# Block sums of a two-level MLP product moved from GpSimd to VectorE in a Hymba-style decoder step

## The reference

```python
def _channel_and_ple(h, mix, p_l, w_out, g_ffn, w_up, w_down, w_ple, w_ple_norm, w_ple_gate):
    h = h + mix @ w_out                                   # 2048 x 2048
    u = _rmsnorm(h, g_ffn)
    h = h + jnp.square(jax.nn.relu(u @ w_up)) @ w_down    # 2048 x 8192, 8192 x 2048
    e = _rmsnorm(p_l @ w_ple, w_ple_norm) * jax.nn.sigmoid(h @ w_ple_gate)
    return h + e
# decode state, 16 heads x 64 x 128 for each of 8 sequences:
    st = st * jnp.exp(d_ * a_gj)[..., None, None] + jnp.einsum('bgjp,bgn->bgjpn', x_ * d_[..., None], b_)
```

## Time and profile before

| | |
|---|---|
| median of 3 runs | 2960.68 us (2950.65 to 2961.87) |
| profiled execution | 2962.45 us, span 2960.7 us |
| output projection ends, first unit starts | 1136 us |
| up projection | 1136.7 to 1994.3 us |
| down projection | 2005.3 to 2722.2 us |
| PLE, gate, final norm | to 2960.7 us |
| busy: PE, DVE, ACT, POOL | 88%, 72%, 38%, 49% |

### The profile page before, as it was taken

How to read it: one execution, slowest core, us unless ns; L and a number is a source line. 1 busy time by engine, 2 the same in 40 slices (tenths; PEclk the granted TensorE clock), 3 DMA queues, 4 the chain that set the end, 5 groups by cost and what they waited for, 6 DMA issues and landing times.

```text
span 2960.7 us, 51598 instructions
## 1 busy us (share of the span) xinstructions
PE 2611.2 (88%) x20223; PEld 2465.4 (83%) x20223; DVE 2144.2 (72%) x2523; ACT 1124.8 (38%) x1845; POOL 1455.2 (49%) x778
## 2 busy tenths in 40 slices
PE   7999999967868997888888888886999999999998
PEld 7999999823447996778878888886999999999998
DVE  4287877457476227898888888885999999998533
ACT  3111111247633223444444444442444444444322
POOL 0098899000072015555555555554666666655322
PEclk9999999987778998899999999998999999999999
DMA  4487888498433331444444444457555655552223
GB/s 127 121 284 258 288 302 272 127 415 310 184 100 123 100 115 53 148 149 160 162 147 151 149 160 149 160 186 274 201 188 191 210 201 194 201 172 79 94 93 115
DMA packets 334327, 526.46 MB, mean 178 GB/s; under 512 B 16421, under 2 KB 257699, under 8 KB 324966
## 3 DMA queue, kind: packets, MB, share of 16 engines
q1 hardware_dynamic: 311096, 510.16, 50.1%
q10 hardware_dynamic: 22990, 13.01, 1.5%
HBM read 442.67 MB, written 80.55 MB: 177 GB/s over the span
## 4 chain that ended last, share of the span: by engine, by line
PE 46%; DVE 19%; POOL 14%; DMA 9%; issue 7%; ACT 3%; SPq 2%; ACTq 0%; POOLq 0%; DVEq 0%
DVE wl L2454 9%; PE ps L1479 7%; PE ps L1481 7%; PE ps L1484 7%; PE ps L1894 7%; PE ps L1896 7%; PE ps L1897 7%; POOL sr L1343 5%; DMA rb<-in_w_up 5%; POOL kpage L1245 5%; POOL tb L1366 2%; DMA kpage<-in_cache_k 1%; DMA vpage<-in_cache_v 1%; ACT wh L1068 1%; DVE hst L2479 1%
## 5 line engine op out<-in xcount | busy, mean ns | idle before, releaser
L1479 PE MATMUL ps<-uh,wh 128*128 128x260 f32 x2464 | 651.6, 285 | 18.4 <-DVE wl L1991 13.8
L1481 PE MATMUL ps<-ul,wh 128*128 128x260 f32 x2464 | 647.6, 284 | 0.0
L1894 PE MATMUL ps<-op,wh 128*128 128x260 f32 x1536 | 461.1, 300 | 129.5 <-DVE wl L2454 117.9
L1991 DVE TENSOR_TENSOR wl<-raw,wh 128x1024 fp32r<-128x1024 f32 (+1 forms) x162 | 254.8, 1573 | 360.7 <-ACT wh L760 360.6
L1484 PE MATMUL ps<-uh,wl 128*128 128x260 f32 x2464 | 497.7, 284 | 0.0
L1479 PEld LDWEIGHTS ps<-uh,wh 128*128 128x128 f32 x2464 | 468.9, 190 | 20.8 <-DVE wl L1991 10.0
L1481 PEld LDWEIGHTS ps<-ul,wh 128*128 128x128 f32 x2464 | 467.8, 190 | 0.0
L1896 PE MATMUL ps<-op,wh 128*128 128x260 f32 x1536 | 454.1, 296 | 0.0
L1897 PE MATMUL ps<-op,wl 128*128 128x260 f32 x1536 | 453.5, 295 | 0.0
L1245 POOL TENSOR_TENSOR kpage<-kpage,qbc 128x1024 f32<-128x1024 f32 x128 | 357.0, 2824 | 159.1 <-DMA kpage<-in_cache_k 158.7
L1894 PEld LDWEIGHTS ps<-op,wh 128*128 128x128 f32 x1536 | 309.5, 201 | 142.3 <-issue 104.1
(11 more groups left out here) (403 smaller groups left out, 5887.0 us busy)
## 6 DMA issues: line engine op xcount, KB each, us to landing
kpage<-in_cache_k SPq DMA_DIRECT2D x128, 512.0 KB, 4.8
vpage<-in_cache_v SPq DMA_DIRECT2D x128, 512.0 KB, 5.8
rb<-in_w_up SPq DMA_DIRECT2D x128, 512.0 KB, 4.5
wb<-in_w_down SPq DMA_DIRECT2D x128, 512.0 KB, 5.3
hid_scr<-hst SPq DMA_DIRECT2D x32, 1820.0 KB, 6.3
raw<-in_w_in SPq DMA_DIRECT2D x88, 512.0 KB, 4.6
ev<-hid_scr SPq DMA_DIRECT2D x28, 1040.0 KB, 7.7
od<-hid_scr SPq DMA_DIRECT2D x28, 1040.0 KB, 7.9
```

Source lines behind the costliest of these rows:

```text
L1479: mm(ps[:, bank + 2 * m + f, 0:HALF], h_, xh[:, f * HALF:(f + 1) * HALF], start=st, stop=False)
L1481: mm(ps[:, bank + 2 * m + f, 0:HALF], h_, xl[:, f * HALF:(f + 1) * HALF], start=False, stop=False)
L1894: mm(out, h_, pairs[:, k, 0, :], start=(opens and first and k == 0), stop=False, skip_group_check=True)
L1991: tt(wl[:, c % 2, 0:elems], raw[:, c % 2, 0:elems], wh[:, c % 2, 0:elems].bitcast(F32), ALU.subtract).then_inc(lo_ready, 1)
```

## The change

All block sums of the MLP (`operand_sum`, `weight_sum`, `down_sum`, `hidden_sums`) and the last sum of squares run on VectorE, placed by `beside(x)` between its other work; GpSimd does nothing from the last group of the output projection until the PLE stage. The decode state's two multiplies become 16 ScalarE copies with a scale of 128 columns each, only the add stays whole and goes to VectorE. The first operands of u are begun before the last slab of the output projection is split, and the order of the operand steps and of units 1 and 2 changes. On SyncE `load_down(0)` is issued one group earlier, the first part's pieces earlier and in the order 0, 1, 4, 5, 2, 3, 6, the last reload of h one step later and in two pieces, and the first `w_ple` loads one step later.

```diff
-        wbuf = [sb("wb0", [2, 4, 256], F32, "RAW"), sb("wb1", [2, 4, 256], F32, "XX", RB)]
+        wbuf = [sb("wb0", [2, 4, 256], F32, "XX", RB), sb("wb1", [2, 4, 256], F32, "RAW")]
@@ SyncE
             for g in range(UPS):
                 for m in (2 * g + 3, 2 * g + 4):
...
+                    elif m == 2 * UPS:
+                        rows_used(m - 3)
+                        load_down(0)
...
+            for i in (0, 1):
+                sp.wait_ge(q_used, X_UP - 14 + 6)
+                load_part(0, i)
             rows_used(2 * UPS - 1)
-            load_down(0)
+            load_down(1)
+            for i in (4, 5, 2, 3, 6):
+                sp.wait_ge(q_used, X_UP - 14 + (6, 6, 10, 10, 8, 8, 12)[i])
+                load_part(0, i)
             store_hidden(UPS - 2)
...
-                if n == 0:
+                if n == 1:
                     store_hidden(UPS - 1)
...
+                if n == 1:
+                    sp.wait_ge(h_st, 16 * 8 + 16 * UPS)
...
@@ ScalarE, beside(x)
+                    if n % 8 in (4, 5):
+                        if n % 8 == 4 and i == 0:
+                            act.wait_ge(u_in, 16 * (c + 2 + c // 4))
+                        for b in ((i,) if i < 6 else (6, 7)):
+                            if n % 8 == 4:
+                                A(stm[:, b], stm[:, b], ACT.Copy, scale=ecol[:, c, b:b + 1]).then_inc(u_s, 1)
+                            else:
+                                A(bxm[:, b], bbm[:, b], ACT.Copy, scale=xdt[:, c, b:b + 1]).then_inc(u_s, 1)
@@ VectorE
+            def weight_sum(g, k):
...
+                if k == 0:
+                    for m in (2 * g, 2 * g + 1):
+                        dve.wait_ge(r_in[m % 3], 32 * (m // 3 + 1))
+                    tt(s1, a21, a22, ALU.add).then_inc(s_sum, 1)
...
+            def hidden_sums(g):
...
+                dve.wait_ge(x_q, g + 1)
+                tt(tb[:, 0:4:3], tm[:, :, HALF:T], halves(tm[:, 0]), ALU.subtract).then_inc(t_h, 1)
+                dve.wait_ge(t_h, 3 * g + 1)
+                tt(tb[:, 1], tm[:, 1, HALF:T], tb[:, 0], ALU.subtract).then_inc(t_h, 1)
+                dve.wait_ge(t_h, 3 * g + 2)
+                tt(tb[:, 2], tm[:, 1, 0:HALF], tb[:, 1], ALU.subtract).then_inc(t_h, 1)
...
+            def state_update(t):
+                dve.wait_ge(u_s, 16 * (t + 1))
+                tt(stm, stm, bxm, ALU.add).then_inc(u_n, 1)
@@ VectorE, beside(x): up projection, g, a = x // 14, x % 14
+                    if x == 7:
+                        weight_sum(0, 1)
+                    if 0 < g < UPS and a == 0:
+                        weight_sum(g, 1)
+                    if g < UPS and (a == 8 or a == 4 and g):
+                        weight_sum(g, 2 + a // 8)
...
-                    if g and a in (9, 10, 11):
-                        hidden_lo(g - 1, a - 9)
+                    if g and a == 9:
+                        hidden_sums(g - 1)
+                    if g and a in (10, 11, 12):
+                        hidden_lo(g - 1, a - 10)
+                    if a == 13 and g < UPS - 1:
+                        weight_sum(g + 1, 0)
+                    elif a == 13 and g == UPS - 1:
+                        down_sum(0, 0)
+                    if x == 6:
+                        last_squares()
+                    if x == 8:
+                        operand_sum(6)
@@ VectorE, beside(x): down projection, n, i = (x - X_UP) // 7, (x - X_UP) % 7
+                    if i in (0, 1, 3):
+                        down_sum(n, (1, 2, 3, 3)[i])
+                    if i == 5 and n + 1 < DOWNS:
+                        down_sum(n + 1, 0)
+                    if n % 8 == 6 and i == 4:
+                        state_update(n // 8)
@@ VectorE, start of the MLP
+            lo(SL_OUT + 30)
+            operand_sum(0)
             operand_lo(0)
+            operand_lo(1)
+            lo(SL_OUT + 31)
+            operand_sum(1)
+            operand_sum(2)
+            operand_lo(2)
+            weight_sum(0, 0)
             unit_lo(0)
             unit_lo(1)
-            operand_lo(1)
             h_out_of(7)
-            operand_lo(2)
+            operand_sum(3)
             operand_lo(3)
+            operand_lo(4)
             unit_lo(2)
             unit_lo(3)
+            weight_sum(0, 2)
+            operand_sum(4)
+            operand_lo(5)
+            operand_sum(5)
             for x in range(4, X_ALL):
-                if x < 14:
-                    operand_lo(x)
+                if x < 12:
+                    operand_lo(x + 2)
                 unit_lo(x)
                 beside(x)
```

More of the change, by code:

```diff
@@ L1372, in state_update @@
-            def state_update(t):
-                pool.wait_ge(u_in, 16 * (t + 2 + t // 4))
-                step(pool.tensor_tensor(stm, stm, ecol[:, t, 0:NB].unsqueeze(2).to_broadcast([P, NB, NS]),
-                                        ALU.mult))
-                step(pool.tensor_tensor(bxm, bbm, xdt[:, t].unsqueeze(2).to_broadcast([P, NB, NS]), ALU.mult))
-                pool.tensor_tensor(stm, stm, bxm, ALU.add).then_inc(u_n, 1)
-            operand_sum(0)
-            operand_sum(1)
-            weight_sum(0, 0)
@@ L1382, in _ @@
-            for k in range(2, 6):
-                operand_sum(k)
-            add_squares(7, 0, None, sqo)
-            weight_sum(0, 1)
-            pool.wait_ge(h_st, 16 * 8)
-            weight_sum(0, 2)
-            operand_sum(6)
-            operand_sum(7)
-            weight_sum(0, 3)
-            for g in range(UPS):
-                if g + 1 < UPS:
-                    weight_sum(g + 1, 0)
-                if g:
-                    hidden_sums(g - 1)
-                if g + 1 < UPS:
-                    for k in range(1, 4):
-                        weight_sum(g + 1, k)
@@ L1399, in _ @@
-            for n in range(DOWNS):
-                for k in range(4):
-                    down_sum(n, k)
-                if n == 0:
-                    hidden_sums(UPS - 1)
-                if n % 8 == 4:
-                    state_update(n // 8)
+            pool.wait_ge(h_rt, 1)
             step(pool.memset(acc, 0.0))
@@ L1857, in residual @@
                                    start=False, stop=False)
-                    mm(ps[:, b + 1, SEQ - HALF:HALF], xs3[0:NB, col:col + P], ident[0:NB, 0:NB],
-                       start=False, stop=False)
+                    z = mm(ps[:, b + 1, SEQ - HALF:HALF], xs3[0:NB, col:col + P], ident[0:NB, 0:NB],
+                           start=False, stop=False)
+                return z
             for g in range(8):
@@ L2435, in h_out_of @@
                 dve.sem_inc(group_free, 1)
-            for g in range(8):
-                for j in range(4 if g < 7 else 2):
+            for g in range(7):
+                for j in range(4):
                     lo(SL_OUT + 2 + 4 * g + j)
-                if g < 7:
-                    h_out_of(g)
+                h_out_of(g)
             def operand_lo(k):
@@ L2507, in h_split, with operand_sum @@
                    ALU.subtract).then_inc(s_ul, 1)
+            def operand_sum(k):
+                n, a, b = ((1, 0, 7), (2, 0, 7), (4, 0, 7), (1, 7, 8), (2, 7, 8), (4, 7, 8), (3, 0, 8))[k]
+                if k == 0:
+                    dve.wait_ge(u_e, 14)
+                    dve.wait_ge(s_kvt, 2 * NH + 1)
+                elif k == 3:
+                    dve.wait_ge(u_e, 16)
+                elif k == 6:
+                    dve.wait_ge(o_t, 4)
+                else:
+                    dve.wait_ge(o_lo, {1: 1, 2: 2, 4: 4, 5: 5}[k])
+                    dve.wait_ge(o_t, k)
+                out, in0, in1 = {1: (t1, b12, b11), 2: (b11, b22, t1), 3: (b12, b22, b12), 4: (t1, b21, b11)}[n]
+                tt(out[:, a:b], in0[:, a:b], in1[:, a:b], ALU.subtract).then_inc(o_t, 1)
@@ new lines, in down_sum @@
+            def down_sum(n, k):
+                w = wbuf[n % 2]
+                a11, a21, a12, a22 = w[:, 0, :, 0:P], w[:, 0, :, P:2 * P], w[:, 1, :, 0:P], w[:, 1, :, P:2 * P]
+                if k == 0:
+                    dve.wait_ge(r_in[1 - n % 2], down_landed(n) + 32)
+                if n == 0 and k == 0:
+                    dve.wait_ge(q_lo, X_UP - 2)
+                elif k == 1:
+                    dve.wait_ge(q_lo, X_UP + 7 * n)
+                elif k > 1:
+                    dve.wait_ge(s_sum, 4 * UPS + 4 * n + (1, 3)[k - 2])
+                out, in0, in1 = ((dring[0], a21, a22), (dring[3], a11, a21), (dring[1], dring[0], a11),
+                                 (dring[2], a12, dring[1]))[k]
+                tt(out, in0, in1, ALU.subtract if k else ALU.add).then_inc(s_sum, 1)
```

213 lines of the change are left out of this document (100 added, 113 removed).

## The result

The changed kernel takes 2706.65 us, median of 4 runs (2704.52 to 2710.84), against 2961.26 us of the kernel before, median of 4 (2950.65 to 2961.87). The ratio is 0.915, 95% interval 0.9126 to 0.9173. The forecast was 2714 us, with a range of 2680 to 2785.

A forecast was written before the change was run, and what follows sets the result against it. It took VectorE and GpSimd, delaying each other's SBUF reads, as the up projection's bound. Stages 1135.9 + 34.4 + 23.9 + 30 x 20.5 + 6.4 + 646 + 14 + 238.5 made 2714 us, range 2680 to 2785.

The forecast's parts named there:

- The mechanism: Up projection: VectorE and GpSimd hold each other up reading SBUF; 128x512 subtraction 0.68 us alone, 2.86 beside a GpSimd sum.
- VectorE's prices by starts: VectorE instructions priced from start to start, not by duration: 0.60 us for 512 columns, 1.13 for 1024.
- The rival without overlap: VectorE instructions don't overlap when it is full: group 22.4 us, down step 10.55, total 2802 us; chance 0.11.
- Up group: Up projection: VectorE 20.3 us with waits against TensorE's 20.2, taken as 20.5; 167 us gained over 31 groups.
- group 1: Up projection's second group: VectorE's reciprocal of 3.39 us is no longer under anything, so it takes 23.9 us.
- over 95%: Sign named for the forecast: VectorE busy over 95% in the up projection.
- Group 0: From the output projection's end to group 1: 34.4 us instead of 50.3, with late rows for group 1; gain 15.9.
- The stop at the change: Before the down projection: 6.4 MB at 426 GB/s plus 3 us latency is 18 us; TensorE stands 6.4 instead of 10.96.
- the second, lower rate: Loads before the down projection: at the Trainium skill's HBM rate of 358 GB/s, 2.9 us more.
- The down projection: TensorE-bound: VectorE 9.2 us a step against 10.09; 646 us plus 14, where 71 us are lost now.
- The 14 us: Down projection's allowances: pieces, hidden store, SyncE, half clock 2, h_split 1.4, state's load 1, changes of part 3.
- Its slack: Down step: VectorE's 9.2 us of work against TensorE's 10.09 leaves 0.9 us to spare.

The follow-up runs named there:

- experiment 1: Changed kernel plus four GpSimd multiplications of 128x1024 in SBUF per group in groups 2 to 30 of the up projection: 2877.21 us, group 26.25 us.
- experiment 2: Kernel with the added GpSimd multiplications beside the up projection, each replaced by two memsets of the same scratch, which only write SBUF: 2712.59 us.
- experiment 3: Changed kernel with the second block sum of up-projection groups 2 to 30 done twice on VectorE: 2738.19 us, group 21.52 us.
- Experiment 9: Changed kernel with each up group's second block sum moved to unit seven: 2704.32 us; with one semaphore per down-projection piece and new load order: 2706.99; both: 2707.45.
- experiment 8: Changed kernel with the first up-projection operands begun behind the last output-projection split, as before the change: 2716.0 us.
- experiment 4: Changed kernel with the second block sum of each down-projection step done twice on VectorE: 2721.63 us, step 10.25 us.
- experiment 6: Changed kernel with the decode state's two multiplications given back to GpSimd, sums and the state's add staying on VectorE: 2725.5 us, median of 2.

## Why the prediction was right, and where its terms were off

- **The mechanism.** That two engines hold each other up in reading SBUF, and that VectorE alone fits beside TensorE, is shown by experiments 1 and 2: four GpSimd operations that read cost 5.87 us a group, eight that write cost nothing. One row was read loosely: the split of 1430.42 in the earlier trace rows wasn't undisturbed. GpSimd's sum of 1430.58 stood beside it; VectorE had begun first and kept its 0.68 us, and GpSimd took 2.79.
- **VectorE's prices by starts** held: 0.60 us for 512 columns and 1.13 for 1024 in full order, and experiment 3 charged 1.14 for the latter. The rival without overlap would have had 22.4 us a group. Here the Trainium skill's sentence in "VectorE: DVE Perf Modes", section "The DRAIN you can't avoid", that the next operation waits for an empty pipe, doesn't agree with these rows. The same paragraph goes on that a next operation that isn't held starts earlier, and with that they agree; the rival rested on the first sentence alone.
- **Up group**: 20.5 forecast, 20.38 measured; over groups 1 to 31 this is 4.3 us less than forecast, with group 1 at 23.0 us for 23.9. VectorE is busy for 94%, where over 95% was named as a sign. VectorE was taken as the bound at 20.3, which experiment 3 confirms, and 0.2 us put on top of it, which wasn't needed. Experiment 9 adds that the bound isn't work but one wait in the order: filled, the group is TensorE's.
- **Group 0**: 34.4 forecast, 36.5 measured. The late rows for group 1 are there (VectorE waits 3.23 us for `rb` at 1158.98), and experiment 8 prices the early operands at 5.3 us of the 13.8 gained.
- **The stop at the change**: 6.4 forecast, 9.9 measured. The mis-sized term is the transfer: the forecast had 18 us from its issue to the first unit, 3 of latency and 6.4 MB at 426 GB/s, and it took 21.4, from 1785.19 (SyncE's issue) to 1806.63. Part of it is the rate. While the up projection still runs the first row below shows 313 GB/s, but this holds 2 us at 146 at the start, the latency, and 404 and 416 GB/s right behind. Only from 1791 to 1797 is it 323, 278 and 358, 0.64 MB less than at 426, or 1.5 us. The other 2 us stay open. The rate over the stop itself, 421 GB/s, is near the 426 taken, so the second, lower rate in the prediction isn't needed. Busy time by stretch, last column GB/s:

```profile
1785.00:1795.00 10.00, 10.00 (x85) 10.00 (x84) 9.65 (x16) 6.52 (x14) 0.00 (x0) 1.00 0.90 313
1795.00:1805.00 10.00, 1.73 (x15) 1.51 (x13) 5.03 (x9) 2.06 (x4) 0.00 (x0) 0.70 1.02 411
```

- **The down projection**: 660 forecast, 657.7 measured, but not for the reason given. I read 717 us over 64 steps as a loss spread over all of them by contention. The usual step of before was at TensorE's 10.09 us already. The loss was in the eight steps with the state (seven of 14.5 to 14.6 us, one of 15.6, 36 us over the usual), in three stops at the beginning (3.87, 2.71 and 10.25 us), and in the last steps. A single step read in order of time would have shown that; the mean of a stage didn't. The forecast came out because it priced the new step and not the old one's cause. The 14 us that it put over TensorE's 646 are 12 in the run, in other parts: 5.3 in the stops of the second and fourth step, about 5 at less than full clock behind the three stops (0.50 from 1806.63 to 1810, 2 forecast), 1.8 in four steps with `h_split` (10.54 us each), and nothing at the changes of part, where 3 were forecast.
- **Its slack**: 0.9 us forecast; experiment 4 shows that 0.60 us of added work costs 0.16 a step. 0.9 was the difference of two sums, and part of it stands as a wait (0.47 us) that the added work didn't fill.
- **The start**: 10.3 us of the 11.2 that the forecast lies above the span of after come from code that nothing changed. The other terms are off by +2.1 (group 0), -4.3, +3.5 and -2.3 us and cancel to 1; that the sum is so close is in part luck.

What is left open: where in the first 1100 us the unchanged code varies, and why, beyond the clock's part; 2 us of the stop at the change; and what holds the 0.47 us in a down step.

## What to carry to other kernels

When an engine's instruction has two durations, look for what runs beside the long one: here moving work onto the busier of two engines took load off both. Price a full engine by the distance of starts and add the waits in its order; an engine at 94% can be the bound, and one added instruction shows whether it is. Before you ascribe a stage's loss to each of its steps, read the steps one by one: a mean of 11.2 us was 10.1 in most, 14.6 in every eighth, and three stops at the beginning.

## What the runs showed of the hardware

- A VectorE instruction with two SBUF inputs that meets a reading GpSimd instruction isn't slowed in proportion but held until that one is done: excesses of 1.24 to 1.71 us for one, and in sum the group's growth. In experiments 1 and 6 each stretched instruction ends 0.54 to 0.56 us behind GpSimd's end. GpSimd is held in the same way: 1.89 us when it goes first, 6.25 for two behind VectorE's.
- Which of the two goes first isn't settled by the start alone. GpSimd's instruction of 1501.15 met a VectorE split that had begun at 1500.92; the next two VectorE instructions (1501.52 and 1502.65) still took their usual time, and by its end GpSimd began at about 1507.40 - 2 x 1.89 = 1503.6, an estimate. The one of 1517.85 met a split of 1517.61 in the same way, and there it went ahead of VectorE's next instruction (2.40 us for 0.69).
- GpSimd's writes cost VectorE nothing: 113 pairs of 0.96 us memsets in 580 us, stage 1311.8 us with and without them (1310.1 in a second execution without).
